# Splits, an embedding copy and a weighted sum reordered in a two-layer decoder trunk

## The chip, the cores and the metric

The kernel runs on one core of one Trainium2 chip. The metric is the device time of one execution, in microseconds. Before the change the median of three runs is 2429.65 us (2429.29 to 2430.94).

## The reference

The input h is 256 tokens by 2048 features, in float32. There are two layers. Layer 0 mixes tokens by a causal convolution module, layer 1 by differential attention (8 heads, two softmaxes for each, their difference applied to v, then a norm over each head). After the mixer each layer has a gated feed-forward part with a causal convolution of width 3 between its products, and then a gated embedding:

```python
h = h + rms_norm(mixer(rms_norm(h, pre_mix_g[i])), post_mix_g[i])
h = h + rms_norm(conv_ffn(rms_norm(h, pre_ffn_g[i]), ...), post_ffn_g[i])
gate = sigmoid(rms_norm(h, ple_pre_g[i]) @ w_gate + b_gate)
h = h + rms_norm(gate * (p[i] @ w_proj), ple_post_g[i])
```

The inner sizes are 4096 for the first product of the convolution module, 6144 for q, k and v, 5632 twice for the feed-forward part, and 256 for the embedding rows p.

## The kernel before

Nearly all products are made from split operands. A float32 matrix becomes a high part (rounded to float32r) and a low part (the difference), and three of the four products of parts are summed on TensorE. ScalarE makes the high part of each weight piece (`split` of ScalarE, L625) and VectorE the low part (`split` of VectorE, L1015). The activations x are split likewise (`x_high`, L655, and `x_low`, L1040).

The weights are streamed in units of 256 rows by 512 columns, through a ring of four buffers `raw`, `w_hi` and `w_lo` (RING = 4). SyncE loads a unit when the low part of the unit four before it is made (L438). The high part of a unit can be made when its piece of `raw` has landed and TensorE has used the unit four before it. `place` numbers all units in the order of use, and one counter, `units_used`, orders the ring. In a token stage (pw2, wo, down, proj, gate) a unit is twelve matmuls of 512 columns (L1634 to L1636); eight units make a chunk of 512 output features. In a feature stage (q and k, up) a unit is eight pairs of matmuls (L1599, L1601).

Each engine follows its own written-out program and the engines meet in counters, so a late instruction holds back everything behind it on its engine. Four stretches are touched.

*Gate stages* (one for each layer, `new_h_behind`). TensorE ends the down product and makes the third and fourth 512 columns of the embedding product (`project(2)`, `project(3)`). The first eight transposes of the new h (`turn_h`, L1579) stand inside `project(3)`, the next eight behind it. It then waits for ScalarE's copy of the third block, runs `keep_warm(WARM, 0)` (five products of the identity, ten instructions, L1691), and starts the gate's first chunk, whose first unit waits for four complete x tiles (`start_with=4`). The last sixteen transposes stand after unit 2. ScalarE copies the third block (`project(0)`), splits unit 2, copies the fourth block (`project(1)`, L968) and only then makes the high parts of x tiles 0 to 3. VectorE, in its own `new_h_behind`, updates four pieces of h, makes x tiles 0 to 3, splits unit 1, makes tiles 4 to 7, splits unit 2, updates the other four pieces of h (L1060), splits unit 3, makes tiles 8 to 11, splits unit 4, makes tiles 12 to 15 and splits units 5 and 6. VectorE's routine also serves the start of layer 1's q and k stage; ScalarE's serves it too, with other copies (L821).

*End of attention* (L1834 and `rest_of_o`). Between the last units of the v product TensorE makes weighted sums, six blocks behind the scores. Before: the last two v units, the transposes of the first quarter of o, a wait for the last quarter of v (copied by ScalarE, L868), the weighted sums of the last four blocks, the transposes of the second quarter, and then unit 0 of wo, which waits for x tiles 0 to 3. ScalarE makes these tiles behind `copy_v(NC - 1)`; VectorE makes them behind the head scaling (L1397) and the last four copies of o (L1383).

*First chunk of pw2* (L815). ScalarE copies two early embedding blocks and then splits units 6 and 7.

*The fetch of `post_mix_g[1]`* (`load_gain`, L565). GpSimd's queue stores the early embedding block, fetches four lambda rows, waits until h is complete, fetches the norm weight to all 128 partitions (1 MB) and makes the attention mask.

Of the kernel before, what the change touches and what calls it, by code (L numbers as in the profile page):

```python
# [29 lines left out]
RING = 4  # L30
# [37 lines left out]
def trunk(nc, t, out):  # L68
# [9 lines left out]
    KT = D // P  # L78
    FT = FF // P
    HALVES = T // P  # L80
    NC = D // UNIT_N
    UPC = KT // UNIT_KT
# [5 lines left out]
    CH_GLU, CH_FFN, CH_QK = D // PAIR_N, FF // PAIR_N, D // PAIR_N  # L88
    ACT_PAIRS = 5
    PE_TAPS = 14  # L90
    WARM_UP, WARM, MIX_WARM, END_WARM = 6, 5, (17, 13), 10
    GRING = 12
    PAIRS = 2 * CH_GLU
    SUMMED = PAIRS - 2
# [168 lines left out]
    with ctx:  # L263
# [277 lines left out]
        def _(pool):  # L541
# [38 lines left out]
            for layer in range(DEPTH):  # L580
                if layer == 1:
                    pool.wait_ge(early_ready, EARLY[0] + EARLY[1])
                    pool.dma_start(z_saved[1][:], z_early[:]).then_inc(early_stored, 16)
                    power(rstd[:], meansq[:], HALVES)
                    for k, n in enumerate(("q1", "k1", "q2", "k2")):
                        pool.dma_start(lam_rows[:, k], t[f"attn_lambda_{n}"][0].partition_broadcast(P)).then_inc(lam_landed, 16)
                    pool.wait_ge(h_updated, PIECES * (ADD["ple0"] + 1))
                    load_gain(t["post_mix_g"][1])
                    nc.gpsimd.memset(mask[:], 0.0).then_inc(pool_consts, 1)
                    pool.wait_ge(pool_consts, 7)  # L590

                    nc.gpsimd.affine_select(out=mask[:, P:T], in_=mask[:, P:T], compare_op=ALU.is_ge, fill=MASK, base=0,
                                            pattern=[[-1, P]], channel_multiplier=1).then_inc(pool_consts, 1)
                    for c in range(NC):
                        mine = slice(HALVES * c, HALVES * (c + 1))
                        power(orstd[:, mine].rearrange("p a b -> p (a b)"), omean[:, mine].rearrange("p a b -> p (a b)"), BPC)
                    power(rstd[:], meansq[:], HALVES)
                power(rstd[:], meansq[:], HALVES)
                if layer == 0:
                    pool.wait_ge(p_turned, 2)  # L600
                    pool.dma_start(p_rows[:], rows_of_p(1)).then_inc(p_landed, 16)
                pool.wait_ge(mid_ready, CH_FFN * (layer + 1) + 1)
                load_gain(t["post_ffn_g"][layer])
                power(rstd[:], meansq[:], HALVES)
                pool.wait_ge(early_stored, 16 * (layer + 1))
                pool.wait_ge(units_used, used(place[f"down{layer}"] + NC * FUPC))
                pool.dma_start(z[:, :, 0:EARLY[layer] * UNIT_N], z_saved[layer][:]).then_inc(early_landed, 16)
                pool.wait_ge(h_updated, PIECES * (ADD[f"ffn{layer}"] + 1))
                load_gain(t["ple_post_g"][layer])
                load_bias(t["ple_b_gate"][layer])  # L610
                power(rstd[:], meansq[:], HALVES)
                power(rstd[:], meansq[:], HALVES)
# [3 lines left out]
        def _(act):  # L616
# [55 lines left out]
                h_squares(left, add, range(PIECES // 2, PIECES))  # L672
                split(None, 0, first + RING + 2, 2)

            def new_h_behind(add, left, scale, first, project):

                project(0)
                split(None, 0, first + 2, 1)
                project(1)
                x_high(left, scale, range(0, 4))  # L680
                split(None, 0, first + 3, 1)
                x_high(left, scale, range(4, 8))
                h_squares(left, add, range(0, 4))
# [109 lines left out]
            def token_stage(name, add, biases=False, done=0):  # L793
# [15 lines left out]
                with act.Fori(0, NC - peeled) as i:  # L809
                    chunk(i, UPC, place[name] + UPC * peeled, lambda: post(i, i + 1 if peeled else i))  # L810

            act.wait_ge(early_made, 1)
            for c in range(EARLY[0]):
                b = 5 - 2 * c
                nc.scalar.copy(z_early[:, :, UNIT_N * c:UNIT_N * (c + 1)], ps[:, b:b + 2]).then_inc(early_ready, 1)  # L815
            token_stage("pw2", "mix0", biases=True, done=2)
            for layer in range(DEPTH):
                if layer == 1:
                    def project_early(c):
# [1 line left out]
                        nc.scalar.copy(z_early[:, :, UNIT_N * c:UNIT_N * (c + 1)],  # L821
                                       ps[:, 4 + 2 * c:6 + 2 * c]).then_inc(early_ready, 1)

                    new_h_behind("ple0", "mix1", lambda kt: col("pre_mix_g", KT + kt), place["qk"], project_early)

                    def qk_chunk(i, c, s, last):
                        per, first = 2 * UPC, place["qk"] + UPC * (c if i is None else 2 + s)
# [60 lines left out]
                        if a > PV_LAG:  # L888
                            o_squares(a - PV_LAG - 1)
                    o_squares(BLOCKS - BPC - 1)  # L890
                    split(None, 0, place["v"] + RING + V_POS[-1], NC * UPC - V_POS[-1])
                    copy_v(NC - 1)
                    x_high("attn", head_gain, range(0, 4))
                    for b in range(BLOCKS - BPC, BLOCKS):
                        o_squares(b)
                    x_high("attn", head_gain, range(4, 12))
# [72 lines left out]

                gain_of = lambda kt: col("ple_pre_g", layer * KT + kt)  # L970
                first = place[f"gate{layer}"]
                new_h_behind(f"ffn{layer}", f"ple{layer}", gain_of, first, lambda c: project(EARLY[layer] + c))
                if layer == 0:
                    p_high(2)

# [27 lines left out]
        def _(dve):  # L1003
# [75 lines left out]
            def new_h_behind(source, left, scale, first):  # L1079
# [6 lines left out]
                x_low(left, scale, range(4, 8))  # L1086
                split(None, 0, first + 2, 1)
                residual(source, range(PIECES // 2, PIECES))
                split(None, 0, first + 3, 1)
                x_low(left, scale, range(8, 12))  # L1090
                split(None, 0, first + 4, 1)
                x_low(left, scale, range(12, KT))
                split(None, 0, first + 5, 2)
                dve.wait_ge(hstats_done, PIECES * (HNORM[left] + 1) + 1)
                inverse_root(hstat, D)
                split(None, 0, first + 7, 1)
# [219 lines left out]
            for layer in range(DEPTH):  # L1316
                if layer == 1:
# [84 lines left out]
                    for a in range(STEPS):  # L1402
# [9 lines left out]
                            head_means(c - 1)  # L1412
                        if c >= 1 and k == 1:
                            head_norm(c - 1)
                    copy_o(BLOCKS - BPC - 1)
                    head_means(NC - 2)
                    split(None, 0, place["v"] + RING + V_POS[-1], NC * UPC - V_POS[-1])
                    head_norm(NC - 2)
                    for b in range(BLOCKS - BPC, BLOCKS):
                        copy_o(b)  # L1420
                    x_low("attn", head_gain, range(0, 4))
                    head_means(NC - 1)
                    x_low("attn", head_gain, range(4, 8))
                    head_norm(NC - 1)
# [129 lines left out]
        def _(pe):  # L1554
# [245 lines left out]
            for layer in range(DEPTH):  # L1800
                if layer == 1:
# [37 lines left out]
                    for a in range(STEPS):  # L1839
# [19 lines left out]
                        if a >= PV_LAG:  # L1859
                            d = a - PV_LAG  # L1860
                            pe.wait_ge(v_ready, d // BPC + 1)
                            pe.wait_ge(w_t_ready, d + 1)
                            if d:
                                pe.wait_ge(o_copied, d)
                            weighted_sum(d, 7)
                    v_units(range(V_POS[-1], NC * UPC))
                    turn(0, range(0, 1))
                    pe.wait_ge(v_ready, NC)
                    pe.wait_ge(w_t_ready, BLOCKS)
                    pe.wait_ge(o_copied, BLOCKS - BPC)  # L1870
                    for b in range(BLOCKS - BPC, BLOCKS):
                        weighted_sum(b, 7 - b % BPC)
                    turn(0, range(1, 2))

                    def rest_of_o(j):
                        if j == 1:
                            pe.wait_ge(o_copied, BLOCKS)
                            turn(0, range(2, 3))
# [49 lines left out]
                project(3, lambda: turn_h(f"ffn{layer}", range(1)))  # L1928
                turn_h(f"ffn{layer}", range(1, NC // 2))
                pe.wait_ge(proj_ready, projected(layer, 3))  # L1930
                keep_warm(WARM, 0)

                def rest_of_h(j):
                    if j == 2:
# [2 lines left out]
                    if j == 5 and layer == 0:  # L1937
                        turn_p(1)

                token_chunk(None, place[f"gate{layer}"], lambda half: ps[:, half], f"ple{layer}", rest_of_h)  # L1940
                if layer == 0:
                    pe.wait_ge(p_ready, 3)
                with pe.Fori(0, NC - 1) as i:
# [34 lines left out]
```

## Time and profile before

| | |
|---|---|
| median of the runs | 2429.65 us |
| the profiled execution's own time | 2430.65 us |
| its span (first to last instruction) | 2428.9 us |
| TensorE busy | 2405.4 us, 99% of the span |
| VectorE busy | 1638.4 us, 67% |
| ScalarE busy | 1237.8 us, 51% |
| TensorE's granted clock | 1.000, mean over the span |
| DMA, mean over the span | 186 GB/s |

The rows say what each engine did and what ended the idle time before an instruction. PE is TensorE, PEld its weight load, DVE is VectorE, ACT is ScalarE, POOL is GpSimd. A number such as L1015 is a line of the kernel before. A start is counted from the start of the span. Several like instructions in a row are merged: the duration is that of the group and xN is their number.

### The profile page before, as it was taken

The page shows a single profiled execution, that of the slowest core. Times are in us where ns is not written, and L with a number is a line of the kernel's source. Part 1 is how long each engine was busy: PE and PEld are TensorE (multiplying, and loading weights), DVE is VectorE, ACT ScalarE, POOL GpSimd, SP SyncE. Part 2 cuts the span into 40 slices and gives each one's busy share as a digit, 9 for nine tenths or more (in the row PEclk, how much of TensorE's full clock was granted, in tenths as well). Part 3 has the DMA queues.
Part 4 walks back from the last instruction along what each step waited for, and adds up shares of the span by engine and source line. Part 5 has one row for each costly group of instructions (what it writes and reads, how often), then busy time and mean ns, then how long its engine had stood idle before and what let it go on. Part 6 is the DMA issues. An engine that isn't in the chain of part 4 may idle for free.

```text
span 2428.9 us, 38855 instructions
## 1 busy us (share of the span) xinstructions
PE 2405.4 (99%) x12392; PEld 2061.9 (85%) x12392; DVE 1638.4 (67%) x2223; ACT 1237.8 (51%) x1777; POOL 36.2 (1%) x65
## 2 busy tenths in 40 slices
PE   9999999999999999999999999999999999999999
PEld 8888788888888888888888887888888888888887
DVE  6999767777777754447755676577777777644465
ACT  3433645555555544446644455465656565444463
POOL 2000000000000000000000000000000000000000
PEclk9999999999999999999999999999999999999999
DMA  8552546656655665556565544656666656655563
GB/s 267 183 166 84 174 147 206 188 181 198 190 186 182 198 213 193 194 184 230 171 223 188 180 156 144 195 156 190 182 189 198 189 179 194 214 189 197 195 222 136
DMA packets 370942, 452.48 MB, mean 186 GB/s; under 512 B 27460, under 2 KB 279494, under 8 KB 369440
## 3 DMA queue, kind: packets, MB, share of 16 engines
q1 hardware_dynamic: 367456, 435.54, 56.2%
q0 software_dynamic: 2960, 15.02, 1.8%
q8 instruction: 44, 0.72, 0.1%
q10 hardware_dynamic: 432, 0.79, 0.1%
q14 instruction: 50, 0.41, 0.1%
HBM read 447.05 MB, written 4.19 MB: 186 GB/s over the span
## 4 chain that ended last, share of the span: by engine, by line
PE 82%; issue 4%; ACT 1%; DVE 1%; DMA 0%; POOL 0%; ACTq 0%; POOLq 0%; SPq 0%; DVEq 0%
PE ps L1599 31%; PE ps L1601 16%; PE ps L1634 11%; PE ps L1636 11%; PE ps L1635 11%; DMA raw<-in_attn_w_qkv 0%; PE ps L1834 0%; PE ps L1579 0%; PE ps L1848 0%; ACT w_hi L625 0%; DVE h L1060 0%; ACT x L655 0%; DVE x L1040 0%; DVE w_lo L1015 0%; ACT vq L784 0%
## 5 line engine op out<-in xcount | busy, mean ns | idle before, releaser
L1015 DVE TENSOR_TENSOR w_lo<-raw,w_hi 128x1024 fp32r<-128x1024 f32 x758 | 923.9, 1224 | 628.9 <-ACT w_hi L625 622.9
L625 ACT CAST w_hi<-raw 128x1024 fp32r<-128x1024 f32 x758 | 790.8, 1049 | 726.4 <-PE ps L1636 369.9
L1599 PE MATMUL ps<-x,w_hi 128*128 128x512 f32 x3328 | 1155.7, 392 | 4.8 <-issue 4.0
L1601 PE MATMUL ps<-x,w_lo 128*128 128x256 f32 x3328 | 931.6, 280 | 0.0
L1599 PEld LDWEIGHTS ps<-x,w_hi 128*128 128x128 f32 x3328 | 622.4, 187 | 142.4 <-issue 5.1
L1601 PEld LDWEIGHTS ps<-x,w_lo 128*128 128x128 f32 x3328 | 628.9, 189 | 0.0
L1636 PE MATMUL ps<-w_hi,mid 128*128 128x512 f32 x704 | 273.9, 389 | 0.0
L1635 PE MATMUL ps<-w_lo,mid 128*128 128x512 f32 x704 | 273.9, 389 | 0.0
L1634 PE MATMUL ps<-w_hi,mid 128*128 128x512 f32 x704 | 273.9, 389 | 0.0
L1634 PE MATMUL ps<-w_hi,x 128*128 128x512 f32 x640 | 253.6, 396 | 5.7 <-DVE x L1040 4.3
L1636 PE MATMUL ps<-w_hi,x 128*128 128x512 f32 x640 | 249.3, 389 | 0.0
L1635 PE MATMUL ps<-w_lo,x 128*128 128x512 f32 x640 | 249.3, 389 | 0.0
L1684 PE MATMUL ps<-xn,wg 128*128 128x256 f32 x896 | 193.7, 379 | 0.0
L1684 PEld LDWEIGHTS ps<-xn,wg 128*128 128x128 f32 x896 | 170.2, 190 | 23.1
L1454 DVE SCALAR_TENSOR_TENSOR acc<-ext,cols,acc 128x256 f32<-128x256 f32 x352 | 147.2, 481 | 46.0 <-ACT acc L925 39.6
L1634 PEld LDWEIGHTS ps<-w_hi,mid 128*128 128x128 f32 x704 | 132.1, 188 | 27.5
L1636 PEld LDWEIGHTS ps<-w_hi,mid 128*128 128x128 f32 x704 | 132.1, 188 | 27.5
L1635 PEld LDWEIGHTS ps<-w_lo,mid 128*128 128x128 f32 x704 | 132.1, 188 | 27.4
L1634 PEld LDWEIGHTS ps<-w_hi,x 128*128 128x128 f32 x640 | 120.2, 188 | 32.5 <-DVE x L1040 4.9
L1636 PEld LDWEIGHTS ps<-w_hi,x 128*128 128x128 f32 x640 | 120.1, 188 | 25.2
L1635 PEld LDWEIGHTS ps<-w_lo,x 128*128 128x128 f32 x640 | 120.2, 188 | 24.6 <-issue 0.2
L1182 DVE SCALAR_TENSOR_TENSOR acc<-u_ext,wconv,acc 128x256 f32<-128x256 f32 x322 | 134.2, 484 | 1.2 <-ACT acc L746 1.1
(193 smaller groups left out, 1308.1 us busy)
## 6 DMA issues: line engine op xcount, KB each, us to landing
raw<-in_ffn_w_in SPq DMA_DIRECT2D x704, 256.0 KB, 3.2
raw<-in_ffn_w_out SPq DMA_DIRECT2D x352, 256.0 KB, 3.3
raw<-in_attn_w_qkv SPq DMA_DIRECT2D x192, 256.0 KB, 2.9
raw<-in_ple_w_gate SPq DMA_DIRECT2D x128, 256.0 KB, 3.6
wg<-in_conv_w_pw SPq DMA_DIRECT2D x112, 256.0 KB, 4.0
raw<-in_conv_w_pw SPq DMA_DIRECT2D x64, 256.0 KB, 3.5
raw<-in_attn_w_o SPq DMA_DIRECT2D x64, 256.0 KB, 3.5
wg<-in_conv_w_pw SPq DMA_DIRECT2D x32, 128.0 KB, 4.2
```

Source lines behind the costliest of these rows:

```text
L625: nc.scalar.copy(w_hi[:, u % RING], raw[:, u % RING]).then_inc(hi_split, 1)
L1015: nc.vector.tensor_tensor(w_lo[:, u % RING], raw[:, u % RING], w_hi[:, u % RING].bitcast(F32), ALU.subtract).then_inc(split_done, 1)
L1182: step.mark(nc.vector.scalar_tensor_tensor(both[:, a], u_ext[:, p, tap:tap + T], wconv[:, tap * KT + p:tap * KT + p + 1], nshift[:] if tap ...
L1454: ins = nc.vector.scalar_tensor_tensor(acc[:, f], ext[:, f, tap:tap + T], col(f"ffn_tap{layer}{tap}", c * 2 + (f if f < 2 else FT + f - 2) ...
L1599: mm(ps[:, 4 * s + f], w_hi[:, u % RING, q, columns], x[:, kt].rearrange("p a t -> p (a t)"), start=kt == 0, stop=False)
L1601: ins = mm(ps[:, 4 * s + f, 0:T], w_lo[:, u % RING, q, columns], x[:, kt, 0], start=False, stop=kt == KT - 1)
L1634: mm(bank(half), hi, w_hi[:, u % RING, q], start=first, stop=False)
L1635: mm(bank(half), hi, w_lo[:, u % RING, q], start=False, stop=False)
L1636: ins = mm(bank(half), lo, w_hi[:, u % RING, q], start=False, stop=last)
L1684: ins = mm(ps[:, 4 * (c % 2) + f, 0:T], wg[:, glu_slot(u), q, P * f:P * (f + 1)], source[:, kt], start=kt == 0, stop=kt == KT - 1)
```

## The change

On TensorE the warm-up matmuls of the gate stages go, and the gate's first unit waits for two x tiles, not four (the second for four). On ScalarE, in the gate stages, the high parts of x tiles 0 to 3 come ahead of the copy of the fourth embedding block. On VectorE the split of unit 4 moves ahead of x tiles 8 to 11, and that of unit 5 alone stays ahead of unit 6's, with tiles 12 to 15 between them. At the end of attention the transposes of the first quarter come ahead of the last two v units, x tiles 0 to 3 ahead of the last v copy and the last copies of o, and unit 0 of wo ahead of the last four weighted sums. In pw2 the splits of units 6 and 7 come ahead of the embedding copies. The fetch of the norm weight waits for the third rescaled q and k chunk.

```diff
@@ gpsimd
-                    pool.wait_ge(h_updated, PIECES * (ADD["ple0"] + 1))
+                    pool.wait_ge(set_free, sets_before["qk"] + 2 + 3)
                     load_gain(t["post_mix_g"][1])
@@ scalar: new_h_behind (turned_early is True for the gate stages, False for q and k)
                 project(0)
                 split(None, 0, first + 2, 1)
-                project(1)
-                x_high(left, scale, range(0, 4))
+                if turned_early:
+                    x_high(left, scale, range(0, 4))
+                    project(1)
+                else:
+                    project(1)
+                    x_high(left, scale, range(0, 4))
                 split(None, 0, first + 3, 1)
@@ scalar: pw2
+            split(None, 0, place["pw2"] + RING + 2, 2)
             act.wait_ge(early_made, 1)
...
-            token_stage("pw2", "mix0", biases=True, done=2)
+            token_stage("pw2", "mix0", biases=True, done=4)
@@ scalar: end of attention
-                    split(None, 0, place["v"] + RING + V_POS[-1], NC * UPC - V_POS[-1])
+                    x_high("attn", head_gain, range(0, 4))
+                    split(None, 0, place["v"] + RING + V_POS[-1], 1)
                     copy_v(NC - 1)
-                    x_high("attn", head_gain, range(0, 4))
+                    split(None, 0, place["v"] + RING + V_POS[-1] + 1, 1)
@@ vector: new_h_behind
                 residual(source, range(PIECES // 2, PIECES))
-                split(None, 0, first + 3, 1)
+                split(None, 0, first + 3, 2)
                 x_low(left, scale, range(8, 12))
-                split(None, 0, first + 4, 1)
+                split(None, 0, first + 5, 1)
                 x_low(left, scale, range(12, KT))
-                split(None, 0, first + 5, 2)
+                split(None, 0, first + 6, 1)
@@ vector: end of attention
                     copy_o(BLOCKS - BPC - 1)
+                    x_low("attn", head_gain, range(0, 4))
                     head_means(NC - 2)
-                    split(None, 0, place["v"] + RING + V_POS[-1], NC * UPC - V_POS[-1])
+                    split(None, 0, place["v"] + RING + V_POS[-1], 1)
                     head_norm(NC - 2)
                     for b in range(BLOCKS - BPC, BLOCKS):
                         copy_o(b)
-                    x_low("attn", head_gain, range(0, 4))
+                    split(None, 0, place["v"] + RING + V_POS[-1] + 1, 1)
@@ tensor: end of attention
+                    pe.wait_ge(v_ready, NC - 1)
+                    turn(0, range(0, 1))
                     v_units(range(V_POS[-1], NC * UPC))
-                    turn(0, range(0, 1))
-                    pe.wait_ge(v_ready, NC)
-                    pe.wait_ge(w_t_ready, BLOCKS)
-                    pe.wait_ge(o_copied, BLOCKS - BPC)
-                    for b in range(BLOCKS - BPC, BLOCKS):
-                        weighted_sum(b, 7 - b % BPC)
-                    turn(0, range(1, 2))

                     def rest_of_o(j):
+                        if j == 0:
+                            pe.wait_ge(v_ready, NC)
+                            pe.wait_ge(w_t_ready, BLOCKS)
+                            pe.wait_ge(o_copied, BLOCKS - BPC)
+                            for b in range(BLOCKS - BPC, BLOCKS):
+                                weighted_sum(b, 7 - b % BPC)
+                            turn(0, range(1, 2))
@@ tensor: gate stages
-                keep_warm(WARM, 0)
...
-                token_chunk(None, place[f"gate{layer}"], lambda half: ps[:, half], f"ple{layer}", rest_of_h)
+                token_chunk(None, place[f"gate{layer}"], lambda half: ps[:, half], f"ple{layer}", rest_of_h, start_with=2)
```

## Rows read from the trace of the kernel before

**Rows 1.** The page, busy time and instructions of each engine.

```profile
PE 2405.4 (99%) x12392; PEld 2061.9 (85%) x12392; DVE 1638.4 (67%) x2223; ACT 1237.8 (51%) x1777; POOL 36.2 (1%) x65
```

**Rows 2.** The list of waits: engine, line, what for; us in total, times, longest.

```profile
ACT w_hi L625 <- DMA raw<-in_attn_w_qkv: 9.5, 4, 8.0
...
PE ps L1634 <- DVE x L1040: 4.3, 3, 1.5
```

**Rows 3.** Timeline, layer 0's gate stage, TensorE: start, duration, instruction [idle before <- releaser].

```profile
1085.52 1.03 PE L1579 MATMUL ps<-ident,h 128*128 128x128 f32 x8
...
1088.65 1.28 PE L1691 MATMUL ps<-ident 128*128 128x128 f32 x10
...
1091.48 0.50 PE L1634 MATMUL ps<-w_hi,x 128*128 128x512 f32 x1 [1.55 <-DVE x L1040]
...
1099.78 1.91 PE L1579 MATMUL ps<-ident,h 128*128 128x128 f32 x16
...
1101.44 0.48 PE L1634 MATMUL ps<-w_hi,x 128*128 128x512 f32 x1
...
1104.03 0.39 PE L1636 MATMUL ps<-w_hi,x 128*128 128x512 f32 x1
...
1104.66 0.47 PE L1634 MATMUL ps<-w_hi,x 128*128 128x512 f32 x1 [0.24 <-DVE w_lo L1015]
```

**Rows 4.** Timeline, same stage, ScalarE.

```profile
1087.98 1.01 ACT L968 COPY z<-ps 128x1024 f32<-128x1024 f32 x1 [1.66 <-PE ps L1636]
...
1088.88 1.57 ACT L655 ACTIVATE x<-ps,cols 128x256 fp32r<-128x256 f32 x4
...
1090.32 1.07 ACT L625 CAST w_hi<-raw 128x1024 fp32r<-128x1024 f32 x1
...
1100.85 3.03 ACT L655 ACTIVATE x<-ps,cols 128x256 fp32r<-128x256 f32 x8 [3.99 <-PE ps L1579]
```

**Rows 5.** Timeline, same stage, VectorE.

```profile
1089.76 1.66 DVE L1040 SCALAR_TENSOR_TENSOR x<-ps,cols,x 128x256 fp32r<-128x256 f32 x4 [3.35 <-ACT x L655]
...
1095.17 2.74 DVE L1060 SCALAR_TENSOR_TENSOR h<-y_kept,rstd,h 128x512 f32<-128x512 f32 x4
...
1103.29 1.22 DVE L1015 TENSOR_TENSOR w_lo<-raw,w_hi 128x1024 fp32r<-128x1024 f32 x1
```

**Rows 6.** Timeline, layer 1's gate stage, TensorE.

```profile
2325.92 0.50 PE L1634 MATMUL ps<-w_hi,x 128*128 128x512 f32 x1 [1.55 <-DVE x L1040]
...
2339.11 0.47 PE L1634 MATMUL ps<-w_hi,x 128*128 128x512 f32 x1 [0.21 <-DVE w_lo L1015]
```

**Rows 7.** Timeline, end of attention, TensorE.

```profile
1481.48 1.03 PE L1564 MATMUL ps<-ident,hn 128*128 128x128 f32 x8
...
1484.00 2.86 PE L1834 MATMUL ps<-v_sb,w_t 128*128 128x256 f32 x12 [1.48 <-ACT v_sb L868]
...
1488.94 0.50 PE L1634 MATMUL ps<-w_hi,x 128*128 128x512 f32 x1 [1.21 <-DVE x L1040]
```

**Rows 8.** Timeline, end of attention, ScalarE and VectorE.

```profile
1482.68 1.26 ACT L868 ACTIVATE v_sb<-ps,rstd 128x512 f32<-128x512 f32 x2
...
1487.23 1.65 DVE L1040 SCALAR_TENSOR_TENSOR x<-ps,lam,x 128x256 fp32r<-128x256 f32 x4
```

**Rows 9.** Timeline, first chunk of pw2, ScalarE and TensorE.

```profile
267.44 1.92 ACT L815 COPY z_early<-ps 128x1024 f32<-128x1024 f32 x2
...
271.88 0.47 PE L1634 MATMUL ps<-w_hi,x 128*128 128x512 f32 x1 [0.99 <-DVE w_lo L1015]
```

**Rows 10.** Timeline, first q and k chunk, TensorE.

```profile
1205.16 0.47 PE L1599 MATMUL ps<-x,w_hi 128*128 128x512 f32 x1 [0.16 <-DVE w_lo L1015]
...
1225.85 0.50 PE L1599 MATMUL ps<-x,w_hi 128*128 128x512 f32 x1 [0.58 <-DVE w_lo L1015]
```

**Rows 11.** Source view of the norm weights' fetch, all six issues.

```profile
DMA to landing us min/median/max: 4.6/8.2/11.1
```

**Rows 12.** Windows view: length, busy of each engine, granted clock, DMA share, GB/s.

```profile
1088.00:1092.00 4.00, 2.45 (x20) 2.22 (x19) 2.24 (x5) 4.00 (x9) 0.00 (x0) 1.00 0.08 33
```

More of the change, by code:

```diff
@@ L90, in trunk @@
     PE_TAPS = 14
-    WARM_UP, WARM, MIX_WARM, END_WARM = 6, 5, (17, 13), 10
+    WARM_UP, MIX_WARM, END_WARM = 6, (17, 13), 10
     GRING = 12
@@ L673, in new_h, with new_h_behind @@
                 split(None, 0, first + RING + 2, 2)
-            def new_h_behind(add, left, scale, first, project):
+            def new_h_behind(add, left, scale, first, project, turned_early):
                 project(0)
                 split(None, 0, first + 2, 1)
-                project(1)
-                x_high(left, scale, range(0, 4))
+                if turned_early:
[4 more added lines that the diff above has]
+                    x_high(left, scale, range(0, 4))
                 split(None, 0, first + 3, 1)
@@ L822, in project_early @@
                                        ps[:, 4 + 2 * c:6 + 2 * c]).then_inc(early_ready, 1)
-                    new_h_behind("ple0", "mix1", lambda kt: col("pre_mix_g", KT + kt), place["qk"], project_early)
+                    new_h_behind("ple0", "mix1", lambda kt: col("pre_mix_g", KT + kt), place["qk"], project_early, False)
                     def qk_chunk(i, c, s, last):
@@ L971, in _ @@
                 first = place[f"gate{layer}"]
-                new_h_behind(f"ffn{layer}", f"ple{layer}", gain_of, first, lambda c: project(EARLY[layer] + c))
+                new_h_behind(f"ffn{layer}", f"ple{layer}", gain_of, first, lambda c: project(EARLY[layer] + c), True)
                 if layer == 0:
@@ L1414, in _ @@
                             head_norm(c - 1)
+                    assert NC * UPC - V_POS[-1] == 2
                     copy_o(BLOCKS - BPC - 1)
+                    x_low("attn", head_gain, range(0, 4))
                     head_means(NC - 2)
-                    split(None, 0, place["v"] + RING + V_POS[-1], NC * UPC - V_POS[-1])
+                    split(None, 0, place["v"] + RING + V_POS[-1], 1)
                     head_norm(NC - 2)
```

## The prediction, made before the changed kernel was run

> **What bounds the kernel now.** I read the page first. TensorE is busy for 99% of the span [rows 1], its mean granted clock is 1.000 (the 2.4 GHz level), and the chain of waits runs mostly through its matmuls. Nothing that the result needs is removed by this change, so only the stretches in which TensorE waits can pay. The second view was therefore the list of waits [rows 2]: it puts 4.3 us, in three places, down to VectorE's low parts of x. The same list has ScalarE waiting 8.0 us once for a piece of attn_w_qkv; that matters only if TensorE feels it. Third came the timelines around every place where TensorE idles, engine by engine, since the instruction that is late there is queued in program order behind others.
>
> A stall costs more than the idle time in brackets. Matmuls overlap: the twelve of a unit start 0.235 us apart ((1104.03 - 1101.44) / 11) but last 0.39, so the next would have started 0.16 us before the end from which the idle time counts. I add 0.16 to each idle figure. Check on the fourth unit of the gate stage: after the start at 1104.03 the next was due at 1104.26 and came at 1104.66, 0.40 late, and 0.24 + 0.16 is 0.40 [rows 3].
>
> **Gate stages, start (twice).** Before: the first eight transposes of h start at 1085.52, and ScalarE makes their high parts only at 1088.88, because in its queue the copy of the second embedding block (1087.98) stands ahead; that copy needs TensorE's last projection matmuls [rows 3, 4]. Meanwhile TensorE runs ten warm-up matmul instructions from 1088.65, then idles 1.55, and starts unit 0 at 1091.48. After: ScalarE can start when the transposes are done. The lag is 1.07 us in the second half of the stage (1099.78 to 1100.85), so the high parts start at 1086.6. VectorE follows 0.88 behind (1088.88 to 1089.76) and does four in 1.66 [rows 5], so two are ready at 1088.4. The start_with of 2 lets unit 0 begin on two. The second group of eight transposes is issued just before 1088.65, where the warm-up now begins; without the warm-up unit 0 starts there. Gain 1091.48 - 1088.65 = 2.83 us. The other stage has the same shape (2325.92, same idle 1.55 [rows 6]): 2.82.
>
> What is late next: the copy of the second block moves from 1087.98 to about 1088.2 (1086.6 + 1.57). Its banks are wanted only by the sixteen transposes after unit 2, so this is hidden. VectorE becomes the thin cover. Its four x end at 1089.1 and unit 1's split (1.22) at 1090.3. ScalarE's copy (0.9) and one split (1.07, of which 0.1 overlaps [rows 4]) put the next high parts at 1090.1, VectorE's four at 1091.0 to 1092.6, the end of unit 2's split at 1093.7 and that of the four pieces of h (2.74 [rows 5]) at 1096.4. TensorE asks for the split at 1094.3 (two units of 12 x 0.235 after 1088.65) and for h at 1097.1: 0.6 and 0.7 us of slack, where h had 1.9 before (1095.17 + 2.74 against 1099.78). I take the full 2.8 each; the ends are 0 (unit 0 waits for four x, and everything slips) and 2.9.
>
> **Gate stages and the stage of attention's q and k, unit 4 (three times).** VectorE's split for unit 4 starts at 1103.29, behind four x that had waited for ScalarE, and ends 0.15 before TensorE's restart at 1104.66 [rows 3, 5]. The diff puts that split right behind unit 3's, at about 1097.6 to 1098.8 by the times above, in an idle stretch of VectorE. Its high part is ready, since ScalarE made it before the second half's x. Unit 5's split now precedes the last four x, which unit 6 wants 5.5 us after unit 4. So the stalls go: 0.40, 0.37 (0.21 + 0.16 [rows 6]) and, in the q and k stage, which uses the same VectorE routine, 0.32 (0.16 + 0.16 [rows 10]). Ends: 0 and the same figures.
>
> **Attention (once).** Before: transposes at 1481.48, an idle 1.48 until ScalarE's copy of the last quarter of v (1482.68) releases the weighted sums at 1484.00, eight more transposes behind these, an idle 1.21 until VectorE's x, which stand at 1487.23 behind the head scaling and four copies of o [rows 7, 8]. After: the first transposes go two units earlier, at about 1475.8; x's first four tiles are made while TensorE runs the last two v units, and wo unit 0 follows at once. That unit (2.8 us) covers the v copy: v ends about 1482.2, the copy needs 1.3 plus a small lag, wo unit 0 ends at 1485.0. The work on TensorE is the same, only reordered. Two idle stretches and their overlaps: 2.69 + 0.32 = 3.0. Next in line are x tiles 4 and 5 for wo unit 2: eight transposes after the sums end near 1488.5, ScalarE and VectorE have them at about 1490.7, and TensorE, with unit 1 and eight transposes in between, asks at 1492. VectorE's split for wo unit 3 is now behind the copies of o, near 1489.5, and asked for at 1495. Ends: 1.5 (if the second wait comes back) and 3.2.
>
> **Last convolution product (pw2).** ScalarE's two embedding copies from 267.44 (1.92 us) stand ahead of the split of unit 6, and TensorE stalls at 271.88, 0.99 idle [rows 9]. Moved ahead, the two splits start at 267.44; VectorE ends unit 6's at about 270.1, before 270.7, when it is asked. Gain 0.99 + 0.16 = 1.15. The copies end near 271.2 instead of 269.3; TensorE wants them only for unit 8 at 276.2, and POOL's store of them starts 1.9 later. Ends: 0 and 1.2.
>
> **The norm weight's fetch.** POOL's 1 MB fetch (four to eleven us to land [rows 11]) is issued amid the q and k stage's first loads, ScalarE's split then waits 8.0 us for weights [rows 2], and TensorE stalls 0.58 idle at 1225.85 [rows 10]. The new wait is on the third rescaled chunk, some 45 us later. Behind it in POOL's queue stand only the mask and the head powers, wanted over 100 us later; the fetched row is for wo's end. Gain 0.58 + 0.16 = 0.74. The four small lambda fetches stay where they are, so the ends are 0 and 0.74; I take 0.7. In steady state there the splits run ahead of TensorE. The same kind of fetch is issued near the start of each down stage, and the list of TensorE's waits has no entry there, so I cost the new place at nothing; without that cover it costs its old 0.74 again.
>
> **Sum.** 2.83 + 2.82 (starts) + 0.40 + 0.37 + 0.32 (unit 4) + 3.0 (attention) + 1.15 (pw2) + 0.7 (fetch) = 11.6. A first matmul after a stall also lasts 0.47 to 0.50 instead of 0.39 [rows 3, 7]; with some of these kept by the transposes I add 0.3 in all: 11.9. The profiled execution took 2430.65 (span 2428.9 and 1.75 around it) and comes to 2418.75; the median run is 1.0 lower, 2429.65, so 2417.8. The likeliest case alone covers 2416.3 to 2419.3.
>
> **The warm-up matmuls.** In the stretch of the gate start TensorE is busy for 2.45 of 4 us, ten warm-up instructions included, and the granted clock is 1.00, the 2.4 GHz level [rows 12]. Without them the waiting goes too, so TensorE has less idle time, not more, and I cost their removal at nothing beyond the gain above. The Trainium skill (TensorE: Matmul & The Clock Gate, Part 1: The HAM clock gate) says that the clock falls back to its lower level when the engine idles and that activity releases it. By that rule too the sum stays 11.9 if the stall is gone; if the x are late in spite of the edit, it speaks against dropping the matmuls, and that is the slower rival below.
>
> **Rivals.**
> - *The cover on VectorE is too thin.* The slack of 0.6 and 0.7 in the gate stages was counted with before's durations; waits between engines add a little at each step. If the transposes after unit 2 or unit 0 itself come 1.5 late in each stage, 3.0 is given back: 2420.8. For it: VectorE would be busy or waiting for ScalarE without a break from 1087.5 to 1096.4. Against: the two gate stages, 1,230 us apart, repeat each other to 0.03 us.
> - *A transfer takes the wait's place.* The fetches of the gate stages and the moved one collide with weight loads that are now asked earlier. For it: the 8.0 us wait for weights. If each of three places costs 1.2, 3.6 goes: 2421.4. Against: in the profile only the fetch at the start of a stage reached TensorE.
> - *The gaps are refilled.* If the weight ring set the pace, TensorE would only wait later: 2429.65. Against: ScalarE's splits mostly wait for TensorE, not the reverse.
> - *Slower: the clock.* Without the warm-up the gate stages begin at 1.2 GHz. At half the clock each unit of 2.8 takes 2.8 longer; the 11.9 is used up after 4.2 such units, and 0.2% (4.9 us, which is what a measurement of this kernel can tell from no change) slower is passed at 6. With four units in each stage it is 22.4 - 11.9 = 10.5 slower: 2440. Against: the clock in rows 12 held through a 1.55 idle stretch.
>
> **How the numbers follow.** Forecast 0.70, thin cover 0.14, transfer 0.08, refilled 0.05, clock 0.03. The first three lie over 0.2% below 2429.65: faster 0.92, same 0.05, slower 0.03. The range takes in both partial cases: above, 2422; below, 2415, with every term at its upper end (0.5 more) and restarts cheaper than I counted.
>
> **What would show it.** Right: unit 0 of each gate stage starts within 0.3 us of the second group of transposes, with no row of warm-up there; unit 4 follows unit 3 without idle; no wait on the v copy and none on x before wo; no idle at pw2's unit 6; the q and k stage without its 0.58; TensorE's waits 7 to 8 us shorter in all. Wrong: a TensorE wait on h or w_lo near the sixteen transposes, a granted clock below 1.00 in those stretches, or a new wait on weights near the moved fetch.

## The result and the profile after

The changed kernel takes 2417.92 us (median of five runs, 2417.44 to 2418.85); the kernel before, run beside it, 2430.94 (2429.29 to 2433.16). The ratio is 0.9945, with a 95% interval of 0.9934 to 0.9956. Forecast were 2417.8 and a range of 2415.0 to 2422.0. One part of the spread, 3 us in one stretch, is shown in the section on the hardware; the two profiled executions both ran without it, and between them the difference is 2430.65 - 2418.1 = 12.55 us.

The page first: TensorE has 6.8 us less busy time, and the span is 12.6 shorter than the 2428.9 of before. Of the 6.8, 2.6 are the twenty warm-up instructions, and 2.3 lie before 246.15, where TensorE waited that much longer for the same work; the rest, about 2, fits the overlapped ends of the stalls and the slower matmuls behind them.

```profile
span 2416.3 us, 38816 instructions
...
PE 2398.6 (99%) x12372; PEld 2057.9 (85%) x12372; DVE 1638.4 (68%) x2223; ACT 1238.3 (51%) x1777; POOL 36.1 (1%) x65
```

The list of waits comes second. These are its rows for TensorE above one microsecond. Before it had 4.3 on VectorE's x, 1.5 on the v copy and 2.1 on VectorE's low parts of weights; none of the three is there any more. What is left are the starts of the three feature stages ("issue"), the transposes of h, one wait for VectorE in the convolution module (vq) and the start of the kernel. The whole list sums to 17.8 before and 12.2 after; at the start of the kernel TensorE waited 2.2 longer in this execution, for x to arrive. That was made up before pw2, as the first mark of the ledger below shows, so 7.8 are gone from the rest.

```profile
PE ps L1607 <- issue: 4.1, 3, 1.4
...
PE ps L1587 <- DVE h L1066: 2.5, 9, 0.6
...
PE ps L1678 <- DMA h<-in_x: 1.8, 1, 1.8
...
PE ps L1699 <- POOL ident L544: 1.5, 1, 1.5
...
PE ps L1763 <- DVE vq L1212: 1.0, 1, 1.0
```

The third view is the timeline of layer 0's gate stage on TensorE, which answers to [rows 3]. The second group of transposes is followed by unit 0 after 0.79 us, with no warm-up between them and no idle time; the sixteen transposes and unit 3 follow without a bracket, and so does unit 4 (no row of TensorE between 1087.41 and 1108 has one).

```profile
1086.62 1.03 PE L1587 MATMUL ps<-ident,h 128*128 128x128 f32 x8
1087.41 0.48 PE L1642 MATMUL ps<-w_hi,x 128*128 128x512 f32 x1
...
1095.68 1.91 PE L1587 MATMUL ps<-ident,h 128*128 128x128 f32 x16
```

ScalarE there ([rows 4]): the four x now start 1.08 after the transposes of 1084.37, and the second block's copy stands behind them.

```profile
1085.45 1.57 ACT L655 ACTIVATE x<-ps,cols 128x256 fp32r<-128x256 f32 x4 [0.28 <-PE ps L1587]
1086.89 1.03 ACT L974 COPY z<-ps 128x1024 f32<-128x1024 f32 x1
...
1088.73 1.60 ACT L655 ACTIVATE x<-ps,cols 128x256 fp32r<-128x256 f32 x4
```

VectorE there ([rows 5]): after its first x, at 1086.32, it waits once, 0.53, until the splits of units 3 and 4 (the row at 1095.00) are done. They now stand ahead of x tiles 8 to 11.

```profile
1086.32 1.66 DVE L1046 SCALAR_TENSOR_TENSOR x<-ps,cols,x 128x256 fp32r<-128x256 f32 x4 [1.07 <-ACT x L655]
...
1089.64 1.66 DVE L1046 SCALAR_TENSOR_TENSOR x<-ps,cols,x 128x256 fp32r<-128x256 f32 x4 [0.53 <-ACT x L655]
...
1092.35 2.73 DVE L1066 SCALAR_TENSOR_TENSOR h<-y_kept,rstd,h 128x512 f32<-128x512 f32 x4
1095.00 2.35 DVE L1021 TENSOR_TENSOR w_lo<-raw,w_hi 128x1024 fp32r<-128x1024 f32 x2
1097.63 1.66 DVE L1046 SCALAR_TENSOR_TENSOR x<-ps,cols,x 128x256 fp32r<-128x256 f32 x4 [0.27 <-ACT x L655]
```

The end of attention on TensorE ([rows 7]): the first transposes now stand at 1470.14, and the last weighted sums and the transposes behind them follow wo's unit 0 without a wait. The copy of v (ScalarE, [rows 8]) ended at 1478.0, under that unit.

```profile
1479.23 2.75 PE L1842 MATMUL ps<-v_sb,w_t 128*128 128x256 f32 x12
1481.81 1.04 PE L1572 MATMUL ps<-ident,hn 128*128 128x128 f32 x8
```

```profile
1476.70 1.27 ACT L873 ACTIVATE v_sb<-ps,rstd 128x512 f32<-128x512 f32 x2 [1.62 <-PE ps L1644]
```

The fetch of the norm weight (GpSimd) starts at 1262.86, and ScalarE's longest wait for q, k and v weights, 8.0 before [rows 2], is 4.9.

```profile
1262.86 0.54 POOL L565 DMA_DIRECT2D gain<-in_post_mix_g  x1 [54.93 <-DVE qk L1336]
```

```profile
ACT w_hi L625 <- DMA raw<-in_attn_w_qkv: 6.1, 2, 4.9
```

The time can be laid out as a ledger: at marks that both timelines have, the distance between the two kernels' starts. Each step of the distance belongs to what lies between two marks. Stretches that the change doesn't touch give steps of -0.16 and 0.03, which tells how fine this ruler is.

| mark on TensorE | before | after | ahead by | step | predicted |
|---|---|---|---|---|---|
| first embedding product, before pw2 | 246.22 | 246.15 | 0.07 | | |
| unit 0 of up, layer 0 (pw2 behind) | 351.20 | 349.89 | 1.31 | 1.24 | 1.15 |
| gate stage 0, first transposes | 1085.52 | 1084.37 | 1.15 | -0.16 | 0 |
| gate stage 0, unit 0 | 1091.48 | 1087.41 | 4.07 | 2.92 | 2.83 |
| q and k, first transposes (unit 4 of the gate behind) | 1187.67 | 1183.09 | 4.58 | 0.51 | 0.40 |
| q and k, spread of the statistic (its unit 4 behind) | 1213.56 | 1208.55 | 5.01 | 0.43 | 0.32 |
| first scores (the fetch's stall behind) | 1378.43 | 1372.56 | 5.87 | 0.86 | 0.7 |
| attention, last transposes | 1500.85 | 1491.82 | 9.03 | 3.16 | 3.0 |
| gate stage 1, first transposes | 2319.97 | 2310.91 | 9.06 | 0.03 | 0 |
| gate stage 1, unit 0 | 2325.92 | 2313.95 | 11.97 | 2.91 | 2.82 |
| last products of h (unit 4 behind) | 2415.42 | 2402.89 | 12.53 | 0.56 | 0.37 |

### The profile page after: what moved, and what is told of

Read it like the earlier page. It is cut to its first block, busy times and chain, and to the rows that moved or that the text cites. A ratio compares the mean times of both kernels' runs of the same rounds, so it can differ in the third digit from the quotient of the medians.

```text
span 2416.3 us, 38816 instructions
## 1 busy us (share of the span) xinstructions
PE 2398.6 (99%) x12372; PEld 2057.9 (85%) x12372; DVE 1638.4 (68%) x2223; ACT 1238.3 (51%) x1777; POOL 36.1 (1%) x65
## 4 chain that ended last, share of the span: by engine, by line
PE 94%; issue 3%; DVE 1%; ACT 0%; DMA 0%; SPq 0%; POOL 0%; ACTq 0%; POOLq 0%; DVEq 0%
PE ps L1607 31%; PE ps L1609 16%; PE ps L1642 12%; PE ps L1643 12%; PE ps L1644 12%; PE ps L1692 9%; PE ps L1587 1%; PE ps L1856 0%; PE ps L1842 0%; DVE h L1066 0%; PE ps L1785 0%; PE ps L1793 0%; DMA h<-in_x 0%; PE ps L1572 0%; POOL rstd L561 0%
```

## The experiments

Eleven kernels ran. The first is the changed kernel itself, each of the others that with one edit. They ran in three series. The first, down to VectorE's split order undone, has a second run of the changed kernel in it; the other two have none, so that their fastest runs can only be set against a fastest run of another series. Since a difference of one microsecond is smaller than the spread of some of them, I give the median, the fastest run, and the distance between marks in the timeline, against the same distance in the changed kernel's; where they differ, the marks decide. The theory is that the gain is a plain sum of stalls removed from TensorE, each worth its idle time and the overlap lost. The rivals are those of the prediction, and that the parts depend on each other.

**The changed kernel again.**

> The changed kernel once more, beside the others of this series. Theory (the gain is the sum of the TensorE stalls removed, 12.5 us in the profile): 2417.9. Rival (part of the 13.0 between the medians was the spread of the kernel before, whose runs lay between 2429.3 and 2433.2): the difference to before comes out at 12 or less, and the changed kernel itself stays within 0.5 of 2417.9.

Median 2421.08, fastest 2418.15 (before beside it: 2433.53, fastest 2429.91); ratio 0.9952 (0.9939 to 0.9966). The median missed both expectations: it is 3 above the 2417.9 of the result. The profiled execution (span 2416.4) keeps all marks within 0.2 of the first one. So one and the same kernel gives medians 3 us apart, and medians can't be compared to a microsecond; what follows rests on marks, with the fastest runs beside them.

**The gate stages' start undone.**

```diff
@@ scalar (False: project(1) ahead of x_high of tiles 0 to 3)
-                new_h_behind(..., lambda c: project(EARLY[layer] + c), True)
+                new_h_behind(..., lambda c: project(EARLY[layer] + c), False)
@@ tensor
+                keep_warm(WARM, 0)
-                token_chunk(..., rest_of_h, start_with=2)
+                token_chunk(..., rest_of_h)
```

> The changed kernel with the gate stages' start put back: the second block's copy ahead of the x tiles on ScalarE, the warm-up matmuls, and four x tiles for unit 0. VectorE's new split order stays. Theory: unit 0 of each gate stage starts 2.9 us later and nothing behind it absorbs that: 2 x 2.9 = 5.8 slower than the changed kernel, 2423.7, with an idle of about 1.5 before unit 0 and none before unit 4. Rival (the early start is partly given back later in the stage, since VectorE's cover had shrunk): less than 4 slower.

Median 2424.84, fastest 2424.25. That is 6.1 above the fastest of the changed kernel in the same series, but only 3.8 by the medians, by which the rival (less than 4) would have it; the marks settle it. From the first transposes to unit 0 it takes 5.95 in gate stage 0 and 5.96 in gate stage 1, against 3.04 in both: 2.9 each. TensorE's timeline has its bracket back before unit 0, and none before unit 4. From unit 0 to the end of the stage it takes 95.67 against 95.68 in gate stage 0 and 89.15 against 88.94 in gate stage 1: at most 0.2 is given back later, and the rival (less than 4) is out.

```profile
1090.32 0.50 PE L1642 MATMUL ps<-w_hi,x 128*128 128x512 f32 x1 [1.54 <-DVE x L1046]
```

**The end of attention undone.**

```diff
@@ tensor
-                    pe.wait_ge(v_ready, NC - 1)
-                    turn(0, range(0, 1))
                     v_units(range(V_POS[-1], NC * UPC))
+                    turn(0, range(0, 1))
...
+                    for b in range(BLOCKS - BPC, BLOCKS):
+                        weighted_sum(b, 7 - b % BPC)
+                    turn(0, range(1, 2))
...
@@ scalar, vector: x_high and x_low of tiles 0 to 3 again behind copy_v(NC - 1) and the last copy_o
```

> The changed kernel with the end of attention put back in the old order on all three engines. Theory: the two idle stretches (about 1.5 and 1.2) return with their overlaps, 3.1 slower than the changed kernel, 2421.0. Rival (the wait on the v copy alone was worth it and the x wait returns elsewhere in the changed order): about 1.7 slower.

Median 2424.26, fastest 2421.46, 3.3 above. From the first scores to up's unit 0 in layer 1 it takes 206.96 against 203.77: 3.19. Both waits are back, in this kernel's list, so the rival (only the wait on the v copy) is out:

```profile
PE ps L1840 <- ACT v_sb L873: 1.5, 1, 1.5
...
PE ps L1640 <- DVE x L1045: 1.2, 1, 1.2
```

**VectorE's split order undone.**

```diff
-                split(None, 0, first + 3, 2)
+                split(None, 0, first + 3, 1)
                 x_low(left, scale, range(8, 12))
-                split(None, 0, first + 5, 1)
+                split(None, 0, first + 4, 1)
                 x_low(left, scale, range(12, KT))
-                split(None, 0, first + 6, 1)
+                split(None, 0, first + 5, 2)
```

> The changed kernel with VectorE's splits of units 3 to 6 in the old order. Theory: unit 4 waits again in both gate stages and in the q and k stage, 0.4 each: 1.2 to 1.4 slower, 2419.2, whatever the start of the stage does. Rival (the stall before unit 4 came from the late start of the stage, and the early start has removed it): no stall at unit 4 in the gate stages, 0.4 from the q and k stage alone, 2418.3.

Median 2422.16, fastest 2419.64, 1.5 above. The stall before unit 4 is back in the gate stages although these start early, 0.24 as in [rows 3], so the rival (it came from the late start) is out. From gate stage 0's sixteen transposes to the q and k stage it takes 87.87 against 87.41: 0.46. By the same kind of marks it is 0.49 in gate stage 1 and 0.58 in the q and k stage.

```profile
1100.22 0.47 PE L1642 MATMUL ps<-w_hi,x 128*128 128x512 f32 x1 [0.24 <-DVE w_lo L1021]
```

**pw2 undone.**

```diff
-            split(None, 0, place["pw2"] + RING + 2, 2)
-            token_stage("pw2", "mix0", biases=True, done=4)
+            token_stage("pw2", "mix0", biases=True, done=2)
```

> The changed kernel with pw2's splits of units 6 and 7 again behind the two embedding copies. Theory: TensorE idles 1.0 before unit 6, 1.2 slower in all, 2419.1. Rival (the later copies hold something else in the changed kernel, so that part of the 1.2 was lost again): 0.6 or less.

Median 2418.86, fastest 2418.77. From pw2's unit 0 to up it takes 97.33 against 96.07: 1.26. Before unit 6 TensorE idles:

```profile
271.36 0.47 PE L1641 MATMUL ps<-w_hi,x 128*128 128x512 f32 x1 [0.97 <-DVE w_lo L1020]
```

**The fetch undone.**

```diff
-                    pool.wait_ge(set_free, sets_before["qk"] + 2 + 3)
+                    pool.wait_ge(h_updated, PIECES * (ADD["ple0"] + 1))
```

> The changed kernel with the norm weight fetched again at the start of the q and k stage. Theory (its megabyte delays the weight pieces beside it): ScalarE waits about 8 us for weights instead of 4.9 and TensorE idles again, 0.7 to 1.2 slower, 2418.9. Rival (the four lambda fetches make the delay, not the norm weight): ScalarE's wait stays near 5 and TensorE has no wait, 2417.9.

Median 2420.30, fastest 2418.07. In its profile TensorE idles 1.80, so with the overlap 1.96 would be lost; the marks give 1.84 (181.70 from the q and k stage's sixteen transposes to the first scores, against 179.86 in the executions of the same pace; the last section tells of the paces). Both are more than the expected 1.2 at most. ScalarE's longest wait is 6.5, less than the 8, but there are more of them.

```profile
ACT w_hi L625 <- DMA raw<-in_attn_w_qkv: 11.8, 6, 6.5
...
PE ps L1607 <- DVE w_lo L1021: 1.8, 1, 1.8
```

So the norm weight's megabyte does cost TensorE time at that place, and how much depends on the execution: 0.86 by the ledger in the profile of before, 1.84 here. The fastest run is only 0.6 above the changed kernel's fastest, 2417.44, which hints at less in some executions; that was not profiled.

**No warm-up and a real idle stretch.** This asks for the clock directly.

```diff
-                new_h_behind(..., lambda c: project(EARLY[layer] + c), True)
+                new_h_behind(..., lambda c: project(EARLY[layer] + c), False)
```

> The changed kernel with ScalarE's copy of the fourth embedding block again ahead of the x tiles, but without the warm-up matmuls and with two x tiles for unit 0. TensorE then stands idle for about 2 us with nothing to fill it. Theory (the granted clock holds through that): unit 0 is 2.1 later in each stage, 4.2 slower, 2422.1, clock 1.00. Rival (the warm-up matmuls kept the clock up): the granted clock falls below 1.00 in the first units, each of which takes up to 2.8 longer, 2425 or more.

Median 2423.07, fastest 2421.93, 4.5 above the changed kernel's fastest. TensorE stands idle for 1.93 before unit 0 and nothing fills it; unit 0 comes 2.96 after the second transposes against 0.79, 2.17 later. The granted clock stays 1.00, the 2.4 GHz level, in that stretch and the next, and the unit's matmuls start 0.23 apart. Gate stage 1 has the same 1.93 and the same clock. So the rival of the lower clock did not come about here, in either stage; that is one profiled execution, and the last section shows one of another kernel in which the clock did fall behind a shorter idle stretch elsewhere.

```profile
1089.42 0.47 PE L1642 MATMUL ps<-w_hi,x 128*128 128x512 f32 x1 [1.93 <-issue]
```

```profile
1087.00:1092.00 5.00, 3.08 (x16) 2.43 (x15) 3.56 (x8) 5.00 (x12) 0.00 (x0) 1.00 0.03 12
1092.00:1100.00 8.00, 8.00 (x45) 6.85 (x44) 7.20 (x11) 4.48 (x13) 1.07 (x2) 1.00 0.61 213
```

**The warm-up kept.**

```diff
+                keep_warm(WARM, 0)
```

> The changed kernel with the ten warm-up instructions left in. Theory (TensorE has no idle time there any more, so they stand on the path): 1.2 longer for each stage less the two tenths that x would be waited for, 2.0 to 2.4 slower, 2420.1. Rival (they fill a wait that is still there): no slower.

Median 2420.18, fastest 2419.57. Unit 0 comes 1.91 after the second transposes against 0.79: 1.12 for each stage, 2.24 in all; the fastest run is 2.1 above the changed kernel's fastest. Once the wait has gone, matmuls that filled it are on the path.

```profile
1087.62 1.28 PE L1699 MATMUL ps<-ident 128*128 128x128 f32 x10
1088.65 0.48 PE L1642 MATMUL ps<-w_hi,x 128*128 128x512 f32 x1
```

**Four x tiles for unit 0.**

```diff
-                token_chunk(..., rest_of_h, start_with=2)
+                token_chunk(..., rest_of_h)
```

> The changed kernel with four x tiles asked for before unit 0 of the gate stages, as before the change. Theory (in the profile of the changed kernel the fourth tile is done 0.6 after unit 0 starts): 0.6 later in each stage, 1.2 to 1.4 slower, 2419.2. Rival (the reordered copy is all of the gain, the tiles are there in time): no slower.

Median 2420.94, fastest 2419.64. From the first transposes to unit 0 it takes 3.71 against 3.04 in both stages: 0.67 each. (The profile puts unit 0's wait down to ScalarE's copy, which ended 0.06 before VectorE's fourth tile; by the code unit 0 waits for the tiles.) Within a gate stage the parts do not add up. Undone alone, the smaller wait costs 0.67, the order on ScalarE 2.17 and the warm-up 1.12, which is 3.96, where all three together gain 2.91: each is worth more with the other two in place. Even so two of them keep something without the third, 0.7 without the new order and 1.8 with the warm-up kept.

**The lambda fetches moved too.**

```diff
+                    pool.wait_ge(set_free, sets_before["qk"] + 2 + 3)
                     for k, n in enumerate(("q1", "k1", "q2", "k2")):
                         pool.dma_start(lam_rows[:, k], ...).then_inc(lam_landed, 16)
-                    pool.wait_ge(set_free, sets_before["qk"] + 2 + 3)
```

> The changed kernel with the four lambda fetches behind the same wait as the norm weight. Theory (they make what is left of ScalarE's wait for weights at the start of the q and k stage, 4.9): that wait falls below 2, and the time stays, since TensorE does not feel it: 2417.9. Rival (the wait is the weight loads' own, asked for late by the order of the splits): 4.9 stays.

Median 2419.25, fastest 2417.57. ScalarE's longest wait for these weights falls from 4.9 to 0.5, so the four lambda fetches made it. TensorE's list has no new entry, and from the q and k stage's sixteen transposes to the first scores it takes 176.85 against 176.86.

```profile
ACT w_hi L625 <- DMA raw<-in_attn_w_qkv: 0.8, 2, 0.5
```

**One step further: the first bank first.** Apart from the start of the kernel, the longest waits left are at the starts of the feature stages.

```diff
-                    pe.wait_ge(x_ready, KT * LEFT[left] + 4)
-                    for j in range(early):
-                        product(j, (0, 1))
+                    pe.wait_ge(x_ready, KT * LEFT[left] + 2)
+                    product(0, (0,))
+                    pe.wait_ge(x_ready, KT * LEFT[left] + 4)
+                    product(0, (1,))
+                    product(1, (0, 1))
```

> The changed kernel with one more edit at the start of the three feature stages (up in each layer, q and k), where the profile still has the three longest waits of TensorE, 1.35 each on x: the part of unit 0 that writes the first bank goes as soon as two x tiles are there (their transposes lie in that bank), the rest at four as before. Theory (the wait is on the third and fourth tile, and two pairs of matmuls, 0.7, fit into it): 0.6 to 0.7 gained in each up stage, under 0.1 in q and k, whose second half waits for eight tiles anyway: 1.3 faster than the changed kernel, 2416.6. Rival (the wait that shows there is for something else, a weight piece or the sequencer): no gain, 2417.9.

Median 2416.57 (four of five runs from 2415.99 to 2417.23), ratio to before 0.9933 (0.9920 to 0.9947). The fastest run is 1.45 under the fastest of the changed kernel (2417.44, in another series), and the "issue" waits fall from 4.1 to 1.7. From layer 0's up, last group of transposes, to the spread of the statistic it takes 20.48 against 21.30: 0.8; from the first scores to layer 1's up it is 0.8 again (202.98 against 203.77), and in the q and k stage it is nothing, as expected. It is the fastest of the kernels here, though its interval overlaps that of the changed kernel, and its profiled execution, 2420.17, ran at the slower pace and lost another 0.9 near 250 us (both in the last section).

```profile
PE ps L1607 <- issue: 1.7, 3, 0.6
```

## Why the prediction was right

**The signs it named** all came: unit 0 right behind the second transposes, unit 4 without idle time, no wait on the v copy, on x before wo or before pw2's unit 6, and the waits 7.8 shorter, where 7 to 8 were forecast.

**The reading of the bound held.** What is gained is the idle time of TensorE that the list of waits and the timelines of before showed, with what a stall costs besides, and nothing took its place. The lead is 12.53 at the last mark, where the prediction had 11.9. Undone one at a time, the gate starts cost 5.83 by the marks, the end of attention 3.19, the split order 1.53 and pw2 1.26, 11.8 together; the ledger has 11.7 for the same four. So between stretches the parts add up, and the rival that they depend on each other is out there.

**That the median came within 0.1 of the forecast is luck.** The forecast of 2417.8 starts from a median of 2429.65; the kernel before, beside the changed one, had 2430.94, and the gain by medians was 13.0, by the profiles 12.55, against 11.9. The gain was therefore forecast 0.6 to 1.1 too low, and in the second run beside the kernel before the changed kernel had its median at 2421.08, inside the range but 3.3 above the forecast. At the start alone executions differ: the first embedding product starts between 245.67 and 247.72 in the thirteen profiles.

**Idle time plus overlap** was the right price, a little low. The rule gave 11.6; the steps that belong to the eight terms sum to 1.24 + 2.92 + 2.91 + 0.51 + 0.43 + 0.56 + 3.16 + 0.86 = 12.6. Each is 0.1 to 0.2 above its term, 1.0 in all, for which I had added 0.3. For unit 4, pw2, attention and the fetch more than half of it is the slower restart: the matmul behind the first one starts 0.30 to 0.33 later, not 0.23. For the gate starts it is something else, since unit 0's first matmul is as slow in the changed kernel (the next starts 0.32 later, before 0.33): unit 0 follows the second transposes by 0.79, where the warm-up followed by 0.87.

**The thin cover** was there and held. VectorE's split for unit 2 ended at 1092.44, and TensorE started that unit at 1092.95; the four pieces of h ended at 1095.08, and TensorE asked for h at 1095.68. The slack was 0.5 and 0.6, where the prediction had 0.6 and 0.7. That rival had the right place and did not come about.

**The warm-up** was costed rightly: removed at no loss, and the runs show both sides, 1.12 per stage if it stays and a clock at 1.00 without it. By the Trainium skill (TensorE: Matmul & The Clock Gate, Part 1: The HAM clock gate) an idle engine gets the lower clock. The trace agrees at the end of the kernel, where it costs nothing: TensorE's last matmul ends at 2411.04, and from 2415 to 2416 the granted clock is 0.50, the 1.2 GHz level. Inside the kernel 1.93 us, the longest idle stretch tried, did not bring it down in the gate stages, but a fall did occur once in thirteen profiles at another place (last section). So the term was right for these executions; that the clock can never fall there is not shown.

```profile
2415.00:2416.00 1.00, 0.00 (x0) 0.00 (x0) 0.00 (x0) 0.00 (x0) 0.00 (x0) 0.50 0.25 88
```

**The fetch** was mis-sized, if anything. Its term was 0.7 with the upper end at the 0.74 that the profile showed; another execution with the fetch at the old place lost 1.84. The upper end should have been open, for one profiled execution gives one draw of a collision between transfers. That the new place costs nothing is shown: in the changed kernel ScalarE waits 0.8 or 1.7 for TensorE at each split from 1259 to 1290, through the fetch at 1262.86, and never for weights.

## What to carry over

When one engine is busy 99% of the span, price a reordering by the list of its waits, and follow each wait to the instruction that stands ahead of the late one in its own engine's queue. In eight of the nine stalls here the late instruction could have run 1 to 6 us earlier; the ninth was a transfer in the way of another. Matmuls that fill a wait must go with the wait, since they are on the path the moment it closes. Edits that close the same wait have to be priced together, since undone one by one they seem to be worth more than they gain. For effects of one microsecond, compare marks within the timelines; medians mix in things that have nothing to do with the edit.

## What the runs showed of the hardware

**Two paces.** One stretch of this program has two paces. In the q and k stage, with the same instructions, no wait on TensorE and a granted clock of 1.00, a window of 120 us holds 694 matmuls in some executions and 681 in others (columns: length, busy time and count of each engine, clock, DMA share, GB/s). First the changed kernel, then the one with attention's end undone, whose edit lies behind this stretch.

```profile
1240.00:1360.00 120.00, 120.00 (x694) 105.80 (x693) 65.16 (x60) 51.93 (x51) 1.34 (x3) 1.00 0.62 198
```

```profile
1240.00:1360.00 120.00, 120.00 (x681) 104.03 (x680) 64.48 (x58) 50.75 (x50) 1.39 (x3) 1.00 0.59 194
```

From the q and k stage's sixteen transposes to the first scores it takes 176.9 us in six of the eleven experiments' profiles (176.85 to 177.05) and 179.86 in three; it takes 180.45 and 181.7 in the two others, which have stalls of their own in it (split order and fetch undone). The slower pace is spread evenly: ScalarE's splits, one for each unit, start 2.83 us apart instead of 2.77. In layer 0's up stage (400 to 800 us) all thirteen profiles have 2309 or 2310 matmuls. The 3 us are the size of the gap between 2418 and 2421 in the changed kernel's runs, and between 2430 and 2433 in those of the kernel before; that it is the same thing there is likely but not shown, since no kernel was profiled at both paces. What sets the pace in an execution stays open: the clock is alike, and the DMA share of the window is 0.59 to 0.64 at the faster pace and 0.58 to 0.61 at the slower. Both paces occur with one and the same program up to the end of this stretch, in the two rows above.

**A fall of the clock inside the kernel.** In twelve of the thirteen profiles the granted clock is 1.00 throughout the work. In the thirteenth, that of the first bank first, it falls to 0.50, the 1.2 GHz level, at 247 us and is back at 1.00 by 251. Before the fall TensorE ran 1-column products of the statistic and idled 1.04, waiting for VectorE; the changed kernel has the same work and the same idle stretch (1.05) there and keeps its clock. The four products that follow take 2.83 instead of 1.96, and pw2 starts about 0.9 later. The edit of that kernel lies behind this place, so it is no effect of the edit. First the kernel with the fall, then the changed kernel.

```profile
244.72 0.70 PE L1765 MATMUL ps<-vq,inv_d 128*128 128x256 f32 x2 [1.04 <-DVE vq L1212]
...
246.07 2.83 PE L1795 MATMUL ps<-w_early,p 128*128 128x512 f32 x4
```

```profile
248.00:250.00 2.00, 2.00 (x7) 1.45 (x6) 1.79 (x5) 1.46 (x2) 0.00 (x0) 0.50 0.00 0
```

```profile
246.15 1.96 PE L1793 MATMUL ps<-w_early,p 128*128 128x512 f32 x4
```

Why it falls in one execution and not in the others stays open. A single profile with the clock at 1.00 therefore does not show that it holds in every execution.
